# SSD step order, rounding ahead of the activation, a fourth un-normalised feed-forward unit, and a pair part first in odd attention

## The chip, the cores and the metric

The kernel runs on one core of a Trainium2 chip. The metric is the device time of one execution in microseconds, and lower is better.

## The reference, cut to what matters

Two blocks follow one another on 16 + 512 tokens of 1024 channels, all in float32. The parts that the change touches:

```python
def rms_norm(x, g):             # every layer begins with it
    return x * rsqrt(mean(x * x, -1) + eps) * g
# SSD layer: h = rms_norm(x, g); z, x, B, C, dt = h @ w_in; a causal convolution of 4 taps
# over x, B and C, then silu; chunks of 128 tokens with decays exp(-cumsum(dt * exp(a_log)));
# y = (state part + inside part + d_skip * x) * silu(z); per group of 512 channels
# y * rsqrt(mean(y * y) + eps) * gate_norm; x + y @ w_out
# feed-forward: h = rms_norm(x, g); u = h @ w_up; a causal convolution of 3 taps over u;
# x + (silu(gate half) * value half) @ w_down
# odd layer of the second block (16 heads, 4 key groups): compressed blocks, selected
# blocks and a window, each a masked softmax, mixed with three gates
```

## The kernel before, in words

**Storage and number format.** Activations stand transposed, channels on partitions, 528 tokens wide (hT, uT and others in one big tile called arena). Each large product is made as three matmuls in a rounded float32 format (`three`, L683 to L685): high weight times high activation, high weight times the rest of the activation, rest of the weight times high activation. A tile of output is 128 channels by 528 tokens, in two halves, so with 1024 input channels it is 8 x 2 x 3 = 48 matmuls.

**Weights.** A weight unit (128 x 2048, two tiles of 128 columns as a rule) is loaded by SyncE into one of HS = 2 raw slots. ScalarE rounds it (`high_part`, L1306, into arena), and GpSimd subtracts to get the rest (`piece` L2345, `rest` L2336, four operations of 512 columns). Where the last tile of unit h is done, ScalarE rounds unit h + 2.

**SSD order.** `ssd_order` (L62) writes out a list of steps by hand, and every engine walks through the same list and does its own share of each step: `pe_step`, `act_step`, `dve_step`, `pool_step`. There are four groups of eight heads. A group has projections B, C and x (four tiles, each with the convolution on VectorE, L1806 to L1815, and a Silu on ScalarE, L1361), z (four tiles, L1831 and Silu L1365), transposes (`bt` L791, `xt` L824), products (`gram` L801, `l0` L807), states (`st`, L832), and per head a `spread` (L817), `decay` (L1908, L1389), `carry` (L1396, L2380) and `weigh` (L1914). Two heads make a `pair` (L839, L843, L848; L1920, L1924), `low` (L1929) splits its result, `ga` and `gs` add up and sum the gate's squares (L1939, L861), `rc` takes the reciprocal (L1944), and `s` is the output projection (L1837, L1839), which runs inside the next group. Tiles go in turn to two pairs of PSUM banks, PS[0] and PS[1], numbered by SSD_M; a step in OFF_TILE uses none. TensorE may start a tile when VectorE or ScalarE has emptied the one two before it.

**Start.** While uT is made, TensorE multiplies dt, then `stat` sums the squares over channels (L755).

**Feed-forward.** A block has halves of 11 units and 22 tiles. The first FIRST = 3 units use the input without its norm, so that they need not wait for the root of the mean square; VectorE multiplies their output by rstd when it empties the bank (L2025). From then on the input is the normalised one (ul2, uh2), which VectorE and ScalarE make in between (`normalised`, L2001, L2005, L1439), and ScalarE empties the banks (L1429). Each unit has two convolutions of 3 taps (L2029, L2032), a Silu (L1435) and a gated product that is split in two (L2036 to L2041).

**Odd attention.** ODD (L189) is a list of parts: for every two heads five `pair` parts, and one `blocks` part (compressed keys, four heads) ahead of two such pairs. Scores run three parts ahead of transposes. For a blocks part VectorE adds a bias and takes maxima (L2250 to L2259), ScalarE takes the exponential, and GpSimd normalises in three operations (L2448, L2450, L2453) before TensorE transposes (L1202). For a pair part the transposes are L1210.

```python
def act_step(what, g, j):
    ...
    elif what in ("B", "C", "x"):
        ...
        act.wait_ge(sem("sconv_full"), n + 1)
        A(dst, ssd["cv"][:, n % 2, :], ACT.Silu)
    ...
    if what in ("B", "C", "x", "z", "s") and last_of_unit((what, g, j)):
        act.wait_ge(ps_full, M + 1)
        high_part("ssd", 0, SSD_UNIT[what, g, j] + HS)
```

## Time and profile before

| | |
|---|---|
| median of 3 runs | 2463.39 us (2460.68 to 2467.31) |
| the profiled execution | 2468.59 us |
| its span, first to last instruction | 2466.5 us |
| TensorE busy | 2274.3 us, 92% |
| VectorE, ScalarE, GpSimd busy | 52%, 37%, 41% |
| mean granted TensorE clock | 0.96 |

The page of the profile gives busy time, waits and the costliest groups of instructions by line. "PE" is TensorE's matmuls, "PEld" its weight loads, DVE is VectorE, ACT is ScalarE, POOL is GpSimd. A busy TensorE is not one at its peak, since matmuls overlap. "<-" names what ended a wait, and a name with a small q (DVEq) is an engine's sequencer, here mostly a drain in front of a signal. The SSD stage lasts from 0 to about 545 us of the span, the first feed-forward block to about 950, the second from about 1274 to 1680, and odd attention from about 2220 to 2400.

### The profile page before, as it was taken

How to read it: one execution, taken by the hardware profiler on the slowest of the kernel's cores; microseconds unless marked ns; L12 is line 12 of the kernel's file. 1: busy time of each engine (PE TensorE's matmuls, PEld its weight loads, DVE VectorE, ACT ScalarE, POOL GpSimd, SP SyncE). 2: the span in 40 equal slices, each digit the busy share in tenths (PEclk: the TensorE clock that was granted, in tenths of full speed). 3: DMA queues.
4: the chain of work that ended last, by engine and by line, in shares of the span. 5: the costliest groups of instructions: out<-in, count | busy, mean ns of one | idle time of the engine just before them, and what ended most of it. 6: DMA issues, size and time to landing. Idle time of an engine off the chain costs nothing.

```text
span 2466.5 us, 38755 instructions
## 1 busy us (share of the span) xinstructions
PE 2274.3 (92%) x15968; PEld 1982.6 (80%) x15968; DVE 1280.1 (52%) x1919; ACT 921.3 (37%) x1480; POOL 1010.0 (41%) x905
## 2 busy tenths in 40 slices
PE   6889899888999999999998999998998899997887
PEld 6778888778999999985598989976785478885665
DVE  6575757588725735234368716732113551016773
ACT  4362626343313333336532323332224431225661
POOL 3252534334545540022244455544345543435751
PEclk9889998989999999999999999999998999998999
DMA  3111112111222222220012222222221011520100
GB/s 154 52 68 53 69 52 69 52 52 69 76 99 93 83 91 95 85 86 1 1 69 70 86 99 97 78 100 74 84 102 70 18 69 69 156 103 35 35 1 34
DMA packets 29373, 175.59 MB, mean 71 GB/s; under 512 B 3984, under 2 KB 4496, under 8 KB 12304
## 3 DMA queue, kind: packets, MB, share of 16 engines
q1 hardware_dynamic: 29200, 173.14, 19.9%
q8 instruction: 126, 2.06, 0.3%
q14 instruction: 47, 0.39, 0.1%
HBM read 166.71 MB, written 2.10 MB: 68 GB/s over the span
## 4 chain that ended last, share of the span: by engine, by line
PE 68%; DVE 9%; POOL 7%; issue 7%; ACT 2%; POOLq 2%; DVEq 2%; SPq 1%; DMA 0%; ACTq 0%
PE PS L683 20%; PE PS L684 19%; PE PS L685 19%; POOL ring_r L2336 2%; PE PS L960 2%; DVE arena L1815 1%; POOL ring_r L2345 1%; POOL arena L2427 1%; POOL arena L2465 1%; ACT arena_r L1306 1%; DVEq L396 1%; POOLq L2462 1%; PE PD L990 1%; POOL uT L2439 1%; PE PC L960 1%
## 5 line engine op out<-in xcount | busy, mean ns | idle before, releaser
L685 PE MATMUL PS<-arena_r,ring_r 128*128 128x264 f32 (+3 forms) x3728 | 1144.9, 307 | 0.0
L2336 POOL TENSOR_TENSOR ring_r<-ring,arena_r 128x512 fp32r<-128x512 f32 (+1 forms) x456 | 596.1, 1337 | 881.3 <-ACT arena_r L1306 881.3
L685 PEld LDWEIGHTS PS<-arena_r,ring_r 128*128 128x128 f32 x3728 | 714.9, 192 | 31.1
L683 PE MATMUL PS<-arena_r,arena_r 128*128 128x264 f32 (+3 forms) x2288 | 691.6, 302 | 25.7 <-issue 8.8
L684 PE MATMUL PS<-arena_r,arena_r 128*128 128x264 f32 (+2 forms) x2256 | 676.1, 300 | 0.0
L683 PE MATMUL PS<-arena_r 128*128 128x264 f32 (+3 forms) x1792 | 566.0, 316 | 22.2 <-DVEq L396 9.3
L683 PEld LDWEIGHTS PS<-arena_r,arena_r 128*128 128x128 f32 x2288 | 435.3, 190 | 53.7 <-issue 25.5
L684 PE MATMUL PS<-uT_r,arena_r 128*128 128x264 f32 (+2 forms) x1472 | 470.0, 319 | 0.0
L684 PEld LDWEIGHTS PS<-arena_r,arena_r 128*128 128x128 f32 x2256 | 429.7, 190 | 13.0 <-issue 0.2
L1306 ACT ACTIVATE arena_r<-ring 128x2048 fp32r<-128x2048 f32 (+1 forms) x146 | 262.0, 1795 | 419.8 <-PE PS L685 404.8
L683 PEld LDWEIGHTS PS<-arena_r 128*128 128x128 f32 x1792 | 348.4, 194 | 50.8 <-issue 21.4
L684 PEld LDWEIGHTS PS<-uT_r,arena_r 128*128 128x128 f32 x1472 | 287.0, 195 | 17.3
L2345 POOL TENSOR_TENSOR ring_r<-ring,arena_r 128x512 fp32r<-128x512 f32 x128 | 176.7, 1408 | 266.1 <-ACT arena_r L1306 266.1
L1972 DVE TENSOR_TENSOR hT<-hT,PS 128x512 f32<-128x512 f32 (+2 forms) x56 | 38.8, 693 | 239.3 <-PE PS L685 239.1
L2032 DVE SCALAR_TENSOR_TENSOR arena<-arena,par 128x528 f32<-128x528 f32 (+1 forms) x176 | 146.2, 831 | 13.1
L1429 ACT ACTIVATE arena<-PS 128x528 f32<-128x528 f32 (+1 forms) x76 | 46.1, 606 | 280.3 <-PE PS L685 280.3
L1718 DVE TENSOR_TENSOR arena<-PS,sd 128x512 f32<-128x512 f32 (+1 forms) x40 | 27.7, 694 | 223.0 <-PE PS L685 222.8
L2029 DVE TENSOR_SCALAR arena<-arena,par 128x528 f32<-128x528 f32 (+1 forms) x88 | 74.7, 848 | 76.6 <-ACTq L396 71.6
L684 PE MATMUL PS<-ring_r,arena_r 128*128 128x256 f32 x352 | 99.8, 284 | 0.0
L685 PE MATMUL PS<-arena_r,uT_r 128*128 128x256 f32 x320 | 91.0, 284 | 0.0
L1631 ACT ACTIVATE arena<-arena 128x128 f32<-128x128 f32 (+3 forms) x128 | 71.1, 556 | 40.2 <-DVEq L396 35.6
L1815 DVE SCALAR_TENSOR_TENSOR arena<-arena,par 128x528 f32<-128x528 f32 x72 | 72.8, 1010 | 5.4
(329 smaller groups left out, 2827.2 us busy)
## 6 DMA issues: line engine op xcount, KB each, us to landing
ring<-stream SPq DMA_DIRECT2D x130, 1024.0 KB, 4.8
ring<-down SPq DMA_DIRECT2D x32, 704.0 KB, 4.0
hT<-x_in SPq DMA_DIRECT2D x4, 528.0 KB, 7.2
arena<-tables SPq DMA_DIRECT2D x4, 512.0 KB, 3.8
arena<-arena SPq DMA_DIRECT2D x16, 128.0 KB, 2.4
out<-uT SPq DMA_DIRECT2D x4, 512.0 KB, 2.8
par<-params SPq DMA_DIRECT2D x1, 1634.5 KB, 13.9
arena<-arena SPq DMA_DIRECT2D x8, 136.0 KB, 3.3
```

What stands on the lines that cost most here:

```text
L683: mm(out_, r32(ah), r32(bh), start=start, stop=False)
L684: mm(out_, r32(ah), r32(b), start=False, stop=False)
L685: return mm(out_, r32(a), r32(bh), start=False, stop=stop)
L960: return mm(sb_z(u, e)[:, a:a + rhs.shape[1]], w, rhs, start=False, stop=True, skip_group_check=True)
L1306: A(r32(high_slot(h)[:, 0:width]), raw_slot(h)[:, 0:width], ACT.Copy).then_inc(sem("high_full"), 1)
L1429: A(ffn[raw][:, FCONV - 1:FCONV - 1 + n], tile_of(stage, 2 * r + m)[:, first_column(n):first_column(n) + n], ACT.Copy)
L1631: A(x, x, ACT.Exp, bias=od["nm"][:, n % 4, i:i + 1], scale=-1.0, accum_out=od["rs"][:, n % 4, i:i + 1])
L1815: last = V.scalar_tensor_tensor(cv, raw[:, k:k + L], w(k), cv, ALU.mult, ALU.add)
L2029: V.tensor_scalar(out_, ffn[raw][:, 0:width], w(0), b, ALU.mult, ALU.add)
L2032: last = V.scalar_tensor_tensor(out_, ffn[raw][:, k:k + width], w(k), out_, ALU.mult, ALU.add)
L2336: last = G.tensor_tensor(r32(low[:, cut]), raw[:, cut], split(high[:, cut]), ALU.subtract)
L2345: last = G.tensor_tensor(r32(low[:, cut]), raw[:, cut], split(high[:, cut]), ALU.subtract)
```

## The change

1. In the first group B runs ahead of `stat`, and dt's product stands in PD, which makes it a step without a tile. z(0,1) runs ahead of l0.
2. At the end of groups 0 to 2, z(g+1,0) and bt(g+1) run ahead of the last pair. Behind it come gram, ga, low, l0, z(g+1,1) and only then gs; rc stands behind xt(1). In the last group z(3,3) runs ahead of the states, and the s tiles are dealt out anew.
3. ScalarE rounds the next weights in front of a step's activation, not behind it (SSD stage only).
4. FIRST is 4. VectorE empties tile 2(r+1) ahead of unit r's gated product and tile 2(r+1)+1 behind it, and makes the normalised input in portions of 4, 2 and 2 channel blocks, where it was 4 and 4.
5. The first two entries of ODD change places, so pair part (0,0) is ahead of the first blocks part; and the sums ahead of the loop are arranged to fit.

```diff
-FIRST = 3
+FIRST = 4
...
+        then = [("z", g + 1, 0), ("bt", g + 1, 0)] if g + 1 < GROUPS else []
...
-        return out + [("pair", g, HPG // 2 - 1)]
+        return out + then + [("pair", g, HPG // 2 - 1)]
...
-    order = [("dt", 0, 0), ("stat", 0, 0)] + projections(0) + [("dtt", 0, 0), ("z", 0, 0), ("end", 0, 0)]
-    order += [("bt", 0, 0), ("gram", 0, 0), ("l0", 0, 0), ("z", 0, 1), ("xt", 0, 0), ("xt", 0, 1), ("xt", 0, 2)]
+    order = [("dt", 0, 0), ("B", 0, 0), ("stat", 0, 0)] + projections(0)[1:] + [("dtt", 0, 0), ("z", 0, 0), ("end", 0, 0)]
+    order += [("bt", 0, 0), ("gram", 0, 0), ("z", 0, 1), ("l0", 0, 0), ("xt", 0, 0), ("xt", 0, 1), ("xt", 0, 2)]
...
-        order += z[0] + [("ga", g - 1, 0), ("low", g - 1, 3), ("bt", g, 0), ("gs", g - 1, 0), ("gram", g, 0), ("l0", g, 0)]
-        order += [("rc", g - 1, 0)] + z[1] + [("xt", g, 0), ("xt", g, 1)] + z[2] + [("xt", g, 2), ("spread", g, 0), ("spread", g, 1)]
+        order += [("gram", g, 0), ("ga", g - 1, 0), ("low", g - 1, 3), ("l0", g, 0)] + z[1] + [("gs", g - 1, 0)]
+        order += [("xt", g, 0), ("xt", g, 1), ("rc", g - 1, 0)] + z[2] + [("xt", g, 2), ("spread", g, 0), ("spread", g, 1)]
+        order += z[3]
         if last:
-            order += [("decay", g, 0)] + states(g, dict(enumerate(s[0:3])))
-            order += through(g, {0: z[3], 1: s[3], 2: s[4], 3: s[5], 5: s[6], 7: s[7]})
+            order += [("decay", g, 0)] + states(g, {0: s[0], 2: s[1]})
+            order += through(g, {0: s[2], 1: s[3], 2: s[4], 3: s[5], 5: s[6], 7: s[7]})
         else:
...
-            order += z[3] + [("decay", g, 0)] + states(g, {0: s[0], 1: s[1] + B, 2: s[2], 3: s[3] + C})
+            order += [("decay", g, 0)] + states(g, {0: s[0], 1: s[1] + B, 2: s[2], 3: s[3] + C})
...
-OFF_TILE = ("spread", "decay", "weigh", "carry", "low", "ga", "gs", "rc", "stat")
+OFF_TILE = ("spread", "decay", "weigh", "carry", "low", "ga", "gs", "rc", "stat", "dt")
...
+ODD[0], ODD[1] = ODD[1], ODD[0]
...
+        dt_sums = PD[:, :, :].rearrange("p a b -> p (a b)")[:, V0:V0 + L]
...
-                            last = mm(t[0:32, V0 + a:V0 + b], w_dt[:, k, :], hT[:, k, a:b], start=k == 0, stop=k == KD - 1)
-                    last.then_inc(ps_full, 1)
+                            last = mm(dt_sums[0:32, a:b], w_dt[:, k, :], hT[:, k, a:b], start=k == 0, stop=k == KD - 1)
+                    last.then_inc(sem("dt_full"), 1)
...
+                if what in ("B", "C", "x", "z", "s") and last_of_unit((what, g, j)):
+                    act.wait_ge(ps_full, M + 1)
+                    high_part("ssd", 0, SSD_UNIT[what, g, j] + HS)
...
-                if what in ("B", "C", "x", "z", "s") and last_of_unit((what, g, j)):
-                    act.wait_ge(ps_full, M + 1)
-                    high_part("ssd", 0, SSD_UNIT[what, g, j] + HS)
...
-                        if half == 0 and r < 2:
-                            for k in range(4 * r, 4 * r + 4):
+                        if half == 0 and r < 3:
+                            for k in range(2 * r + 2 if r else 0, 2 * r + 4):
                                 act.wait_ge(sem("n_raw"), 8 * i + k + 1)
                                 A(r32(uh2[:, k, 0:n], NORMED), sq[:, k % 2, 0:n], ACT.Copy).then_inc(sem("nh_full"), 1)
...
-                    dve.wait_ge(ps_full, dt_M + 1)
-                    V.tensor_tensor(dtv, PS[dt_M % 2][0:32, V0:V0 + L], rstd[0:32, :], ALU.mult)
+                    dve.wait_ge(sem("dt_full"), 1)
+                    V.tensor_tensor(dtv, dt_sums[0:32, :], rstd[0:32, :], ALU.mult)
...
-                    signal(dve, sem("dtv_full"), ps_free[dt_M % 2])
+                    signal(dve, sem("dtv_full"))
...
                         V.tensor_tensor(GA, squares(g, 0), squares(g, 1), ALU.add)
+                        dve.drain()
...
+                def scale(r, m):
+
+                    dve.drain()
+                    tile_wait(dve, f"ffn{i}a", 0, 2 * R, 2 * r + m)
+                    v0 = first_column(width)
+                    V.tensor_tensor(ffn[("rawg", "rawv")[m]][:, FCONV - 1:FCONV - 1 + width],
+                                    tile_of(f"ffn{i}a", 2 * r + m)[:, v0:v0 + width], rstd[:, 0:width], ALU.mult)
+                    signal(dve, free_of(f"ffn{i}a", 2 * r + m))
+
+                scale(0, 0)
...
+                        early = half == 0 and r + 1 < FIRST
...
@@ -2018,19 +2034,16 @@
                             n = raw_tile(i, half, r, m)
                             if n >= 0:
                                 dve.wait_ge(raw_full, n + 1)
-                            else:
-                                dve.drain()
-                                tile_wait(dve, stage, 0, 2 * R, 2 * r + m)
-                                v0 = first_column(width)
-                                V.tensor_tensor(ffn[raw][:, FCONV - 1:FCONV - 1 + width],
-                                                tile_of(stage, 2 * r + m)[:, v0:v0 + width], rstd[:, 0:width], ALU.mult)
-                                signal(dve, free_of(stage, 2 * r + m))
+                            elif (r, m) == (0, 1):
+                                scale(r, m)
                             out_ = ffn[cv][:, 0:width]
                             V.tensor_scalar(out_, ffn[raw][:, 0:width], w(0), b, ALU.mult, ALU.add)
                             for k in range(1, FCONV):
                                 dve.drain()
                                 last = V.scalar_tensor_tensor(out_, ffn[raw][:, k:k + width], w(k), out_, ALU.mult, ALU.add)
                             last.then_inc(conv_full, 1)
+                        if early:
+                            scale(r + 1, 0)
...
-                        if half == 0 and r < 2:
-                            normalised(4 * r)
-                            normalised(4 * r + 2)
+                        if early:
+                            if r == 0:
+                                normalised(0)
+                            scale(r + 1, 1)
+                            normalised(2 * r + 2)
...
-            odd_sum(0)
-            for n in range(2):
-                odd_scale(n)
+            odd_scale(0)
+            odd_sum(1)
```

The order in the boundary from group 0 to group 1 on VectorE. L1920 and L1924 are the last pair, L1831 empties a z tile, L1939 is ga, L1865 and L1867 are gram, L1872 l0, L1944 the reciprocal. Before:

```order
L1933 TENSOR_TENSOR arena<-arena 128x528
L1920 SCALAR_TENSOR_TENSOR arena<-arena,par,PS 128x528
L1924 TENSOR_TENSOR arena<-arena 128x528
L1831 TENSOR_TENSOR arena<-PS,sd 128x528
L1939 TENSOR_TENSOR arena<-arena 128x528 x2
L1929 SCALAR_TENSOR_TENSOR arena_r_51<-arena,par,arena_r_51 128x528
L1865 TENSOR_TENSOR arena<-PS,par 16x16
L1867 TENSOR_TENSOR arena<-PS,par 128x512
L1872 TENSOR_TENSOR arena<-PS,arena 16x128
L1876 TENSOR_SCALAR arena<-arena 16x128
L1944 RECIPROCAL arena<-arena 128x528
```

And now (the same lines are 4 or 5 higher: L1835 z, L1924 and L1928 the pair, L1869 and L1871 gram, L1944 ga, L1876 l0):

```order
L1937 TENSOR_TENSOR arena<-arena 128x528
L1835 TENSOR_TENSOR arena<-PS,sd 128x528
L1924 SCALAR_TENSOR_TENSOR arena<-arena,par,PS 128x528
L1928 TENSOR_TENSOR arena<-arena 128x528
L1869 TENSOR_TENSOR arena<-PS,par 16x16
L1871 TENSOR_TENSOR arena<-PS,par 128x512
L1944 TENSOR_TENSOR arena<-arena 128x528 x2
L1933 SCALAR_TENSOR_TENSOR arena_r_51<-arena,par,arena_r_51 128x528
L1876 TENSOR_TENSOR arena<-PS,arena 16x128
L1880 TENSOR_SCALAR arena<-arena 16x128
L1835 TENSOR_TENSOR arena<-PS,sd 128x528
```

The emptying of z went ahead of the last pair, gram went ahead of ga, and the reciprocal left this place.

The rounding (L1306 before, L1311 now) on ScalarE in the middle of group 0, beside the Silu of tile x(1,1) (L1361, now L1370), with the exponentials of a decay (L1389, now L1398) behind. Before:

```order
L1389 ACTIVATE arena<-arena 128x128 x4
L1396 ACTIVATE arena<-PC 128x512
L1361 ACT_TABLE_LOAD
L1361 ACTIVATE arena<-arena 128x528
L1306 ACTIVATE arena_r_52<-ring 128x2048
L1389 ACT_TABLE_LOAD
L1389 ACTIVATE arena<-arena 128x128 x4
L1396 ACTIVATE arena<-PC 128x512
```

And now:

```order
L1398 ACTIVATE arena<-arena 128x128 x4
L1405 ACTIVATE arena<-PC 128x512
L1311 ACTIVATE arena_r_52<-ring 128x2048
L1370 ACT_TABLE_LOAD
L1370 ACTIVATE arena<-arena 128x528
L1398 ACT_TABLE_LOAD
L1398 ACTIVATE arena<-arena 128x128 x4
L1405 ACTIVATE arena<-PC 128x512
```

The rounding went ahead of the load of the Silu's table and of the Silu.

The first unit of a feed-forward block on VectorE. L2025 (now L2020) empties a tile times rstd, L2029 and L2032 (now L2040 and L2043) are the convolution, L2036 to L2041 (now L2049 to L2054) the gated product, L2001 and L2005 (now L2006 and L2010) the normalised input. Before:

```order
L2025 TENSOR_TENSOR arena<-PS,sd 128x528
L2029 TENSOR_SCALAR arena<-arena,par 128x528
L2032 SCALAR_TENSOR_TENSOR arena<-arena,par 128x528 x2
L2036 TENSOR_TENSOR arena<-arena 128x528
L2039 CAST arena_r_51<-arena 128x528
L2041 TENSOR_TENSOR arena_r_51<-arena,arena_r_51 128x528
L2001 SCALAR_TENSOR_TENSOR sq<-hT,par,sd 128x528 x2
L2005 TENSOR_TENSOR arena_r_53<-sq,arena_r_53 128x528 x2
L2001 SCALAR_TENSOR_TENSOR sq<-hT,par,sd 128x528 x2
L2005 TENSOR_TENSOR arena_r_53<-sq,arena_r_53 128x528 x2
L2025 TENSOR_TENSOR arena<-PS,sd 128x528
```

And now:

```order
L2020 TENSOR_TENSOR arena<-PS,sd 128x528
L2040 TENSOR_SCALAR arena<-arena,par 128x528
L2043 SCALAR_TENSOR_TENSOR arena<-arena,par 128x528 x2
L2020 TENSOR_TENSOR arena<-PS,sd 128x528
L2049 TENSOR_TENSOR arena<-arena 128x528
L2052 CAST arena_r_51<-arena 128x528
L2054 TENSOR_TENSOR arena_r_51<-arena,arena_r_51 128x528
L2006 SCALAR_TENSOR_TENSOR sq<-hT,par,sd 128x528 x2
L2010 TENSOR_TENSOR arena_r_53<-sq,arena_r_53 128x528 x2
L2020 TENSOR_TENSOR arena<-PS,sd 128x528
L2006 SCALAR_TENSOR_TENSOR sq<-hT,par,sd 128x528 x2
L2010 TENSOR_TENSOR arena_r_53<-sq,arena_r_53 128x528 x2
```

Tile 2 is emptied ahead of the gated product, where it was emptied behind all four blocks of normalised input, and tile 3 between the two portions.

## Rows read from the trace of the kernel before

**Rows 1.** The page, its first part: busy time, share of the span, instructions

```profile
PE 2274.3 (92%) x15968; PEld 1982.6 (80%) x15968; DVE 1280.1 (52%) x1919; ACT 921.3 (37%) x1480; POOL 1010.0 (41%) x905
```

**Rows 2.** Busy time by stage: stretch, length, each engine, granted clock, DMA

```profile
0.00:545.00 545.00, 463.55 (x3608) 424.50 (x3608) 366.02 (x474) 253.72 (x371) 211.18 (x156) 0.93 0.19 68
545.00:625.00 80.00, 71.67 (x539) 70.89 (x540) 65.72 (x73) 22.69 (x25) 31.41 (x20) 0.92 0.20 72
625.00:1270.00 645.00, 638.66 (x4954) 580.65 (x4953) 305.70 (x424) 237.38 (x388) 218.75 (x240) 1.00 0.21 72
```

**Rows 3.** TensorE's waits: line, releaser, us in total, times, longest

```profile
PE PC L1202 <- POOL arena L2453: 16.9, 4, 7.4
PE PS L683 <- DVEq L396: 15.9, 12, 4.1
...
PE PC L861 <- DVE arena L1939: 13.4, 4, 4.0
PE PS L683 <- POOL ring_r L2345: 10.8, 4, 5.7
...
PE PS L839 <- DVE arena L1920: 4.7, 3, 2.1
```

**Rows 4.** Busy time in a stretch of the feed-forward at full clock

```profile
612.00:625.00 13.00, 13.00 (x110) 13.00 (x109) 9.84 (x10) 3.80 (x4) 6.17 (x4) 1.00 0.31 108
```

**Rows 5.** Timeline of the start: start, us, engine and line, [idle before <-releaser]

```profile
25.04 2.13 PE L755 MATMUL PC<-sd,par 128*128 128x264 f32 x4 [8.37 <-DVEq L398]
...
37.63 1.28 ACT L1361 ACT_TABLE_LOAD   x1
38.92 0.65 ACT L1361 ACTIVATE arena<-arena 128x528 f32<-128x528 f32 x1
...
45.40 1.90 ACT L1306 ACTIVATE arena_r<-ring 128x2048 fp32r<-128x2048 f32 x1
...
53.67 0.39 PE L683 MATMUL PS<-arena_r 128*128 128x264 f32 x1 [2.60 <-POOL ring_r L2345]
```

**Rows 6.** Timeline, l0's matmuls

```profile
82.09 1.84 PE L807 MATMUL PS<-acs_parts,pick 96*128 96x16 f32 x8 [3.74 <-DVEq L396]
```

**Rows 7.** Timeline, a pair in the middle of group 0

```profile
155.32 1.97 PE L843 MATMUL PS<-arena 128*64 128x128 f32 x16 [2.84 <-DVE arena L1914]
...
159.10 1.98 PE L848 MATMUL PS<-arena 128*64 128x128 f32 x16 [1.81 <-POOL arena L2380]
```

**Rows 8.** Timeline, the boundary from group 1 to 2

```profile
287.75 1.98 PE L843 MATMUL PS<-sq,arena 128*64 128x128 f32 x16 [1.11 <-DVE sq L1914]
...
298.36 2.31 DVE L1939 TENSOR_TENSOR arena<-arena 128x528 f32<-128x528 f32 x2 [0.28 <-issue]
...
300.82 1.64 PE L861 MATMUL PC<-arena,par 128*128 128x264 f32 x4 [2.93 <-DVE arena L1939]
```

**Rows 9.** Timeline, an s tile in the last group

```profile
474.92 0.59 PE L683 MATMUL PS<-arena_r,arena_r 128*128 128x264 f32 x1 [5.66 <-POOL ring_r L2345]
```

**Rows 10.** Timeline, the first feed-forward block's start

```profile
571.06 0.56 PE L683 MATMUL PS<-arena_r 128*128 128x264 f32 x1 [4.14 <-DVEq L396]
...
588.63 0.56 PE L683 MATMUL PS<-arena_r,arena_r 128*128 128x264 f32 x1 [4.16 <-issue]
```

**Rows 11.** Busy time there: up to the first normalised tile; one unit

```profile
551.50:588.60 37.10, 28.83 (x223) 28.43 (x223) 32.59 (x39) 13.15 (x14) 12.64 (x8) 0.95 0.16 58
570.10:581.80 11.70, 10.74 (x76) 10.77 (x77) 10.05 (x11) 1.63 (x2) 6.43 (x4) 0.85 0.23 90
```

**Rows 12.** Timeline, odd attention's first transposes

```profile
2237.61 1.09 PE L1202 MATMUL PC<-par,arena 128*128 128x128 f32 x4 [7.39 <-POOL arena L2453]
```

**Rows 13.** Busy time in a stretch at the lower granted clock

```profile
420.70:431.10 10.40, 10.40 (x49) 9.73 (x48) 4.62 (x5) 3.58 (x4) 0.00 (x0) 0.51 0.21 86
```

**Rows 14.** The convolution's instruction: its group on the page, and durations

```profile
L1815 DVE SCALAR_TENSOR_TENSOR arena<-arena,par 128x528 f32<-128x528 f32 x72 | 72.8, 1010 | 5.4
...
L1815 DVE SCALAR_TENSOR_TENSOR arena<-arena,par x72: 768/770/1667, 35.1 to 410.2; 128x528 f32<-128x528 f32 x72
```

1 line of the change is left out of this document (removed).

## The prediction

> **What bounds it now.** I read the page's totals first, then a table by stage, then TensorE's waits, then the places of the longest. TensorE is busy 92% of a span of 2466.5 us [rows 1], and the stages differ: from 625 to 1270 us it is idle 6 of 645 us at a granted clock of 1.00. In the SSD stage (0 to 545) it is busy 463.6 of 545 at 0.93, and in the first 80 us of the feed-forward block 71.7 at 0.92 [rows 2]. So TensorE sets the end wherever work is there for it, and what the change can win is its idle time, plus what the lower clock behind idle time costs. VectorE is a near second only in the feed-forward start: 65.7 of 80 us. The waits with a cause that repeats are a sum over channels that VectorE hands over late (L861, four times, 13.4 us), weights that GpSimd has not split yet (L683 behind L2345, 10.8), PSUM tiles that VectorE has not emptied (L683 behind a drain, 15.9), and attention's first transposes (L1202) [rows 3]. The change aims at all four.
>
> The profiled execution took 2468.59 us, 5.2 over the median of 2463.39. The sum is made against the profiled one, and the same difference is then taken from the median. A measurement of this kernel can tell about 0.3%, 7 us, from no change.
>
> **Part 1, the start.** TensorE waits 8.37 us in front of the statistics' matmul, while VectorE makes uT piece by piece. Tile B needs just these pieces and fits into that wait; its last piece is there less than a microsecond before the sum is. The statistics then come about half a microsecond later, and C, x0 and x1 move up by a tile, which is 48 matmuls at 13/110 = 0.12 us, with its start 5.9 us [rows 4]. The gain does not arrive whole: banks are emptied behind the dt chain. What decides is x2, which starts at 53.67 behind GpSimd's split, and that behind ScalarE's rounding at 45.40, which waited for C's Silu. B's Silu ends at 39.6 [rows 5]; with the rounding in front of C's Silu and half a microsecond for the later statistics it starts at 40.1, and x2 5.3 us earlier. dt's sum in a bank of its own costs nothing: that bank is not used before the decays. **5.3 us.**
>
> **Part 2, z(0,1) in front of l0.** TensorE idles 3.74 us until VectorE has split the running sums into three parts [rows 6]. A z tile of 5.9 us now stands there, its weights the same unit as z(0,0)'s. **3.7 us.**
>
> **Part 3, rounding in front of the Silu.** In the middle of group 0 a pair waits 2.84 us for a weigh step, whose exponentials stood behind a rounding, and then 1.81 for a carry product that stood on GpSimd behind a split [rows 7]. The rounding needs the tile and not its convolution, so it comes up to a convolution earlier, about 3 us (three L1815 of 0.77 [rows 14] and one scaling). The second wait goes, and the first shrinks by the 1.9 us of the rounding: **3.5**. Groups 1 and 2 wait 2.1 us each for the pair's bank (L839, 4.7 us in three) [rows 3], behind convolutions that run beside a split; a split that is over earlier may free them or hit others, so I take half: **2.0**, bounds 0 and 4.2.
>
> **Part 4, the boundaries.** Three times TensorE waits for the gate's sum, 13.4 less the last group's 3.5, and, in two groups, 1.11 us inside the last pair [rows 3, 8]. Now z(g+1,0) and bt stand in front of that pair, which hides the 1.11. Between the pair and the sum stood z and bt, 6.7 us; now gram, l0 and z(g+1,1) stand there, about 9, and ga (L1939, 298.36) no longer stands behind the emptying of z on VectorE. Both together cover the 2.93 us, and nearly the longest, 4.0. So 9.9 + 2.2 = **12.1**. The reciprocal, 3.45 us on VectorE, moves behind xt(1), where z2's matmuls cover it; without that cover z3's bank would come late by its length. ScalarE gets one table load more, 1.28 us (37.63), and its next activation starts 0.01 us behind it (38.92) [rows 5]: beside TensorE's work, nothing. The last group's sum keeps its wait, since its tail is not reordered.
> The Trainium skill (ScalarE: Activation LUTs, What ACT_TABLE_LOAD costs) adds a drain of about 1.38 us to every switch. By that the added load would take 2.7 us of ScalarE; the row behind the load shows no such time.
>
> **Part 5, last group.** z(3,3) moves ahead of the states, so its unit's rounding is no longer late, and the wait of 5.66 us for a split goes [rows 9]. Late next is the first pair's decay and carry, with three s tiles (3 us each, half a z) above it where z, s and the wait stood; I see no new wait over 1 us. **5.7 us.**
>
> **Part 6, feed-forward, twice.** TensorE waits 4.14 us for an emptied bank and then 4.16 for bank and normalised input [rows 10]. Tile 2 ends at 561.0 (571.06 - 4.14 - 5.9) and is now emptied at once, not at 570.9, so the first wait goes. The second needs VectorE's work counted. Up to the end of normalising it does eight scales, six convolutions, three gatings and four normalised pairs, before it five, four, two and four: 32.6 us busy of 37.1. One unit with two scales, two convolutions and gating is 10.05 [rows 11], a further scale 0.7, so 43.4 us; at the same share busy 49 us, up to 601. TensorE could be at the last piece of the ninth tile at 566.9 + 4.9 x 5.9 = 596. Following both queues, I get 1.3 us of wait at tile 6, 2.3 and 0.6 at tile 8 and about 1 at tile 10, whose rounding stands behind the last copies on ScalarE: 5.2 us in place of 8.3, and about 1 less if a split meets fewer of the operations. **4 each, 8.0**; bounds 0 and 8.3 each. From the fifth unit on nothing changes.
>
> **Part 7, attention.** The first transposes wait 7.39 us for GpSimd's three operations of a "blocks" part [rows 12]. With pair (0,0) in front, its transposes and the next scores, some 3.5 us, run first; but the blocks chain starts behind pair 0 on VectorE, about 1 us later. **2.5 us**, bounds 0 and 6.
>
> **The clock.** Behind such waits the granted clock falls to its lower level, 1.2 of 2.4 GHz: 0.51 from 420.7 to 431.1, behind the third gate sum, where 49 matmuls take 10.4 us, 0.21 each [rows 13]. Eleven stretches of this kind lie behind waits named above, 54 us together. At half speed, with TensorE at some 87% in them, they cost 23. Where waits of 1 to 2 us stay it may still fall; I take half: **12 us**.
>
> **The sum.** 5.3 + 3.7 + 5.5 + 12.1 + 5.7 + 8.0 + 2.5 = 42.8 of idle time and 12 of clock: 54.8. Every cover that is used up bares what is late next. Now ten short waits of about 0.8 us stand in front of L683 for banks alone (15.9 less 4.1 and 4.0) [rows 3]; I take as many new ones off, 8 us. That is 47: a span near 2420, and a median of 2463.4 - 47 = **2416 us**.
>
> **Rivals.**
> - **Collision: slower.** L1815 takes 770 ns alone and up to 1667 beside GpSimd [rows 14]. Its mean of 1010 (72.8 us in 72) says that (1010 - 770)/0.90 = 19 of 72 were hit. The rounding in front puts the split onto the same tile's convolution. If all 72 and the 32 weigh steps are hit, VectorE gets 85 x 0.90 = 76 us more. It goes slower once 61 of the 85 lie on TensorE's path, the price of the 54.8; with all of them the time is 2463 + 76 - 55 = 2484. Against it: the splits are as many as before, moved by 3 us in a rhythm of two tiles, 12 us, and convolutions now cost TensorE 2 us a group. 4%.
> The Trainium skill (SBUF — State Buffer, SBUF: two separate sides) speaks against the change here: the port pair is an exclusive lock, so a VectorE operation with two SBUF inputs waits for the whole GpSimd instruction that holds it. The trace agrees in kind (1667 against 770), and doesn't say how many would meet.
> - **Given back: no change.** 50 of the 85 on the path (45 us) and part 6 lost: 2463 - 55 + 45 + 8 = 2461. 4%.
> - **VectorE bounds the feed-forward start, and the clock stays low.** Parts 6 and 7 and the clock give nothing: 42.8 - 10.5 - 8 = 24, time 2439. For it: VectorE at 82% there [rows 2]. 17%.
> - **All waits go and the clock holds.** 42.8 + 12 (the bounds of parts 3, 6) + 23, with no new waits: 78, time 2385. 11%.
> - Forecast: 64%, its own range 2400 to 2432.
>
> The range that leaves out no more than 2 in 10 is 2391 to 2445. Faster by over 0.3%: 92%; within it: 4%; slower: 4%.
>
> **What would show it.** B's matmuls in the place of the 8.37 us wait and x2 near 48; no wait over 1 us at the l0 matmuls; the gate sum without a wait three times, and the fourth with 3.5 still; no wait over 2 us for a split; the first wait gone in each feed-forward block, with waits of 1 to 3 us at tiles 6, 8 and 10; the transposes' wait near 4; L1815's mean under 1150 ns; the mean clock up from 0.96 to about 0.97. It is wrong if L1815's mean passes 1300 with waits behind L1806 and L1831, or if a feed-forward start still loses 8 us.

## The result, and the profile after

The changed kernel takes **2442.28 us** (median of four runs, 2435.57 to 2444.41) against 2462.98 for the kernel before (median of four, 2460.68 to 2467.31): ratio 0.9912, 95% interval 0.9892 to 0.9932. That is 20.7 us faster. The time lies inside the forecast range (2391 to 2445), but the gain is less than half of the 47 us that were forecast.

The profiled execution of the changed kernel took 2435.57 us, 6.7 under its median; that of before took 2468.59, 5.2 over its own. The two profiles therefore differ by 33 us and the medians by 21. Twelve of the 33 are the two executions and not the change. One execution of the kernel e12_front_two_groups below took 3128 us at a granted clock of 0.65 and is left out of its median.

Line numbers have moved: L683 is now L688, L839 is L844, L843 is L848, L861 is L866, L1815 is L1819, L1929 and L1933 (the low half and the gate's first sum) are L1933 and L1937, and L2345 is L2359. The page's first part, for [rows 1]:

```profile
PE 2260.2 (93%) x15968; PEld 1969.5 (81%) x15968; DVE 1298.7 (53%) x1923; ACT 920.6 (38%) x1477; POOL 1019.2 (42%) x905
```

The table by stage, for [rows 2] (stretch, length, each engine's busy time, granted clock, DMA):

```profile
0.00:522.12 522.12, 451.44 (x3608) 413.94 (x3608) 380.38 (x474) 256.14 (x372) 220.32 (x156) 0.97 0.20 71
522.12:602.00 79.88, 73.41 (x546) 72.23 (x547) 68.27 (x75) 21.86 (x24) 30.78 (x20) 0.92 0.22 80
602.00:1245.00 643.00, 636.68 (x4951) 579.82 (x4950) 306.14 (x425) 237.17 (x387) 219.02 (x240) 1.00 0.20 71
```

The SSD stage went from 545 to 522.1 us with the same 3608 matmuls. TensorE's idle time there (length less busy time, as everywhere below) fell from 81.5 to 70.7 us, so 10.8, and its busy time from 463.6 to 451.4, so 12.1: that is the granted clock, 0.93 before and 0.97 now. VectorE is busy 14.4 us *more* in the stage, for 474 instructions as before.

TensorE's waits up to 522 us, for [rows 3] (line, releaser, us in total, times, longest):

```profile
PE PS L688 <- DVEq L399: 14.4, 12, 2.3
PE PS L844 <- DVEq L401: 9.9, 3, 4.2
...
PE PC L866 <- DVE arena L1944: 3.5, 1, 3.5
PE PS L844 <- DVE arena L1924: 3.3, 3, 2.4
PE PS L688 <- POOL ring_r L2359: 3.3, 3, 1.3
```

Most of what was to go has gone. Of four waits for the gate's sum the last is left (3.5 us). The waits for a split fell from 10.8 to 3.3 us, and the 3.74 us at l0 and the 8.37 us at the statistics are no longer there. (In the middle of group 0, 2.4 and 1.1 us are left of the 2.84 and 1.81 in [rows 7].) But there is a new group, second in size: L844, the first matmuls of the last pair of a group, 9.9 us in three. Before, the last pair waited for its bank 2.1 us each in groups 1 and 2 and 0.5 in the last (L839 in [rows 3]), behind the pair product; now it is 2.8, 4.2 and 2.8 in groups 0, 1 and 2, behind another step. The longest, at the boundary from group 1 to 2, in the timelines of TensorE, VectorE and GpSimd (start, us, engine, line, [idle before it]):

```profile
284.81 0.29 PE L844 MATMUL PS<-arena 16*64 16x16 f32 x4 [4.24 <-DVEq L401]
...
275.33 0.71 DVE L1810 TENSOR_TENSOR arena<-PS,sd 128x528 f32<-128x528 f32 x1
276.16 0.55 DVE L1816 TENSOR_SCALAR arena<-arena,par 128x528 f32<-128x528 f32 x1
276.79 3.33 DVE L1819 SCALAR_TENSOR_TENSOR arena<-arena,par 128x528 f32<-128x528 f32 x3
280.05 1.77 DVE L1933 SCALAR_TENSOR_TENSOR arena_r<-arena,par,arena_r 128x528 fp32r<-128x528 f32 x1
281.74 1.76 DVE L1937 TENSOR_TENSOR arena<-arena 128x528 f32<-128x528 f32 x1
283.57 0.71 DVE L1835 TENSOR_TENSOR arena<-PS,sd 128x528 f32<-128x528 f32 x1
...
278.04 6.58 POOL L2359 TENSOR_TENSOR ring_r<-ring,arena_r 128x512 fp32r<-128x512 f32 x4 [1.65 <-ACT arena_r L1311]
```

Read it backwards. The pair waits for its PSUM bank. The banks go in turn, and in the new order its bank is that of z(2,0), two steps earlier. z(2,0) is emptied at 283.57 (L1835), because VectorE first has x3's convolution, the low half of pair 2 and the gate's first sum to do. These three ran beside a GpSimd split, and three instructions took 1.65 to 1.77 us instead of 0.70 to 0.77. The split starts 1.3 us behind the convolution's first instruction at 276.79, since the rounding in front of x3's Silu released it; with the rounding behind the Silu it starts 5.0 us behind it (below, 280.59 against 275.58).

A second new wait, 2.24 us in group 1 and 2.25 in group 2, comes the same way. The C tile's convolution meets a split, 4.20 us for three instructions instead of 2.46, and the emptying of an s tile stands behind it on VectorE:

```profile
233.51 0.36 PE L688 MATMUL PS<-arena_r,arena_r 128*128 128x264 f32 x1 [2.24 <-DVEq L399]
...
225.23 4.20 DVE L1819 SCALAR_TENSOR_TENSOR arena<-arena,par 128x528 f32<-128x528 f32 x3
...
225.68 6.78 POOL L2359 TENSOR_TENSOR ring_r<-ring,arena_r 128x512 fp32r<-128x512 f32 x4 [0.81 <-ACT arena_r L1311]
```

### The profile page after: what moved, and what is told of

Its sections match the earlier page's. It is cut to its first block, busy times and chain, and to the rows that moved or that the text cites. A ratio compares the mean times of both kernels' runs of the same rounds, so it can differ in the third digit from the quotient of the medians.

```text
span 2433.6 us, 38757 instructions
## 1 busy us (share of the span) xinstructions
PE 2260.2 (93%) x15968; PEld 1969.5 (81%) x15968; DVE 1298.7 (53%) x1923; ACT 920.6 (38%) x1477; POOL 1019.2 (42%) x905
## 4 chain that ended last, share of the span: by engine, by line
PE 63%; DVE 13%; issue 7%; POOL 6%; DVEq 3%; ACT 3%; POOLq 2%; SPq 1%; DMA 0%; ACTq 0%
PE PS L688 19%; PE PS L689 18%; PE PS L690 18%; DVE arena L1819 3%; POOL ring_r L2350 2%; PE PS L965 2%; DVE arena L2043 1%; POOL arena L2441 1%; POOL arena L2479 1%; POOLq L2476 1%; DVEq L399 1%; PE PD L995 1%; ACT arena_r L1311 1%; POOL uT L2453 1%; PE PC L965 1%
## 5 line engine op out<-in xcount | busy, mean ns | idle before, releaser
L688 PE MATMUL PS<-arena_r,arena_r 128*128 128x264 f32 (+3 forms) x2224 | 674.2, 303 | 25.5 <-DVEq L399 10.3
L689 PE MATMUL PS<-arena_r,arena_r 128*128 128x264 f32 (+3 forms) x2192 | 658.6, 300 | 0.0
L688 PE MATMUL PS<-arena_r 128*128 128x264 f32 (+3 forms) x1856 | 580.7, 313 | 22.9 <-DVEq L399 8.0
L689 PE MATMUL PS<-uT_r,arena_r 128*128 128x264 f32 (+3 forms) x1536 | 485.9, 316 | 0.0
L688 PEld LDWEIGHTS PS<-arena_r,arena_r 128*128 128x128 f32 x2224 | 423.5, 190 | 54.3 <-issue 30.5
L1311 ACT ACTIVATE arena_r<-ring 128x2048 fp32r<-128x2048 f32 (+1 forms) x146 | 262.2, 1796 | 465.7 <-PE PS L690 451.4
L689 PEld LDWEIGHTS PS<-arena_r,arena_r 128*128 128x128 f32 x2192 | 418.1, 191 | 12.9 <-issue 0.2
L688 PEld LDWEIGHTS PS<-arena_r 128*128 128x128 f32 x1856 | 356.8, 192 | 52.7 <-issue 22.2
L689 PEld LDWEIGHTS PS<-uT_r,arena_r 128*128 128x128 f32 x1536 | 296.5, 193 | 17.3
L2359 POOL TENSOR_TENSOR ring_r<-ring,arena_r 128x512 fp32r<-128x512 f32 x128 | 187.3, 1492 | 219.3 <-ACT arena_r L1311 219.3
L2043 DVE SCALAR_TENSOR_TENSOR arena<-arena,par 128x528 f32<-128x528 f32 (+1 forms) x176 | 158.4, 900 | 13.5 <-issue 0.4
L2040 DVE TENSOR_SCALAR arena<-arena,par 128x528 f32<-128x528 f32 (+1 forms) x88 | 78.4, 891 | 66.6 <-ACTq L399 62.2
L1819 DVE SCALAR_TENSOR_TENSOR arena<-arena,par 128x528 f32<-128x528 f32 x72 | 80.1, 1112 | 5.4
## 6 DMA issues: line engine op xcount, KB each, us to landing
par<-params SPq DMA_DIRECT2D x1, 1634.5 KB, 14.1
```

What stands on the lines that cost most here:

```text
L688: mm(out_, r32(ah), r32(bh), start=start, stop=False)
L689: mm(out_, r32(ah), r32(b), start=False, stop=False)
L1311: A(r32(high_slot(h)[:, 0:width]), raw_slot(h)[:, 0:width], ACT.Copy).then_inc(sem("high_full"), 1)
L1819: last = V.scalar_tensor_tensor(cv, raw[:, k:k + L], w(k), cv, ALU.mult, ALU.add)
L2040: V.tensor_scalar(out_, ffn[raw][:, 0:width], w(0), b, ALU.mult, ALU.add)
L2043: last = V.scalar_tensor_tensor(out_, ffn[raw][:, k:k + width], w(k), out_, ALU.mult, ALU.add)
```

## The experiments

Two theories stood at the start. **T**: the saved time came back as waits for banks behind VectorE's queue in front of the last pair. **R**: the rounding in front moved GpSimd's splits onto VectorE's work just where a bank is wanted. **C** was the rival that it was all clock and luck of the run. All kernels were timed beside the kernel before, in three batches (its medians in them 2461.92, 2464.05 and 2460.95 us). "Idle" is TensorE's idle time up to the first feed-forward statistics, from the table of busy time; before has 81.5. (The expectations count it differently: that of e1_again without the first 7.9 us of the program, the later ones without the last wait, 4.2 us.) e1 to e4, e5 to e8 and e9 to e12 shared a batch each. Where kernels of two batches are compared, the difference is given by the medians and by the ratios. The intervals of e2, e6, e7 and e8 overlap that of e1_again, so for these the idle time has to bear the reading out.

| kernel | us | ratio to before, 95% | idle |
|---|---|---|---|
| e1_again | 2439.99 | 0.9903, 0.9886 to 0.9920 | 71.2 |
| e2_round_behind | 2432.26 | 0.9881, 0.9862 to 0.9899 | 66.0 |
| e3_boundary_old | 2451.63 | 0.9956, 0.9940 to 0.9972 | 75.5 |
| e4_low_behind | 2430.53 | 0.9866, 0.9847 to 0.9885 | 64.4 |
| e5_front_start_only | 2426.19 | 0.9842, 0.9819 to 0.9866 | 62.8 |
| e6_ffn_old | 2444.26 | 0.9910, 0.9889 to 0.9932 | 71.3 |
| e7_start_old | 2445.17 | 0.9920, 0.9901 to 0.9940 | 76.2 |
| e8_odd_old | 2438.47 | 0.9896, 0.9876 to 0.9917 | 69.1 |
| e9_low1_behind_pair | 2426.05 | 0.9851, 0.9827 to 0.9874 | 62.9 |
| e10_rounding_alone | 2465.82 | 1.0013, 1.0000 to 1.0027 | 81.1 |
| e11_boundary_alone | 2443.59 | 0.9925, 0.9906 to 0.9943 | 68.1 |
| e12_front_two_groups | 2428.00 | 0.9861, 0.9835 to 0.9886 | 62.7 |

### The changed kernel again (no edit)

> The changed kernel once more, unedited, for its idle time and its clock in a second profile. Theory T (the idle time that the new order saved at the boundaries came back as waits of TensorE for PSUM banks behind VectorE): the idle time in front of TensorE's matmuls up to the feed-forward statistics is the same as in the first profile, 62 to 64 us, with the last pair of groups 0, 1 and 2 waiting about 10 us together; time 2439 to 2445. Rival C (it is the clock: its gain came in the first profile by luck of that run): the idle time is the same too, but the granted clock of the whole span is 0.965 or less and the stretch that the change does not touch, 350 us behind the first feed-forward start, is as long as in the kernel before.

Measured: 2439.99 us, 22 below before. The idle time is 71.2 (70.7 in the first profile) and the three pairs wait 9.9 us again. The middle stage, which the change does not touch, took 643.63 us here, exactly as long as in the profile of before, and 641.95 in the first profile of the changed kernel (three rows of the table by stage: this run, the first profile, before):

```profile
605.95:1249.58 643.63, 637.32 (x4943) 579.45 (x4942) 305.11 (x423) 236.36 (x387) 218.88 (x240) 1.00 0.21 71
...
602.90:1244.85 641.95, 635.63 (x4943) 578.77 (x4942) 305.32 (x423) 236.21 (x387) 219.02 (x240) 1.00 0.20 71
...
626.83:1270.46 643.63, 637.29 (x4942) 579.28 (x4942) 304.78 (x423) 236.42 (x387) 218.75 (x240) 1.00 0.20 71
```

So C holds for a part of the first profile, and only of it: the whole span's clock is 0.967, where C asked for 0.965 or less. In this profile TensorE's busy time in the SSD stage is 454.6, 9.0 below before: most of the clock's share is real.

### The rounding back behind the activation

The same three lines, taken from the head of ScalarE's step and put at its end:

```diff
-                if what in ("B", "C", "x", "z", "s") and last_of_unit((what, g, j)):
-                    act.wait_ge(ps_full, M + 1)
-                    high_part("ssd", 0, SSD_UNIT[what, g, j] + HS)
...
+                if what in ("B", "C", "x", "z", "s") and last_of_unit((what, g, j)):
+                    act.wait_ge(ps_full, M + 1)
+                    high_part("ssd", 0, SSD_UNIT[what, g, j] + HS)
```

> The changed kernel with the rounding of the next weights back behind the activation (part 3 undone, all else kept). Theory T: the convolution's mean (now 1.11 us) hardly moves, the last pair of three groups still waits 8 us or more, and the waits of 2.8 and 1.8 in the middle of group 0 come back: 2 to 6 us slower than the changed kernel. Rival R (the rounding in front puts GpSimd's split on the same tile's convolution, and this is what filled the saved time): the convolution's mean falls to about 1.01, the last pairs' waits fall from 9.9 to under 4, and the time is 3 to 8 us below the changed kernel's.

Measured: 2432.26 us, 7.7 **faster** than the changed kernel measured beside it (5.4 by the ratios), with 5.2 us less idle time. R's numbers came: the convolution's mean fell from 1112 to 989 ns and the last pairs' waits from 9.9 to 2.0 us. One part of the change costs more than it brings. The same place in this kernel, the boundary from group 1 to 2:

```profile
272.77 0.36 PE L688 MATMUL PS<-arena_r 128*128 128x264 f32 x1 [2.21 <-DVE arena L1924]
...
280.64 0.29 PE L844 MATMUL PS<-arena 16*64 16x16 f32 x4 [1.25 <-DVEq L401]
...
263.97 5.06 DVE L1819 SCALAR_TENSOR_TENSOR arena<-arena,par 128x528 f32<-128x528 f32 x3
...
275.58 2.46 DVE L1819 SCALAR_TENSOR_TENSOR arena<-arena,par 128x528 f32<-128x528 f32 x3
277.95 0.76 DVE L1933 SCALAR_TENSOR_TENSOR arena_r<-arena,par,arena_r 128x528 fp32r<-128x528 f32 x1
278.63 0.70 DVE L1937 TENSOR_TENSOR arena<-arena 128x528 f32<-128x528 f32 x1
...
262.30 6.17 POOL L2359 TENSOR_TENSOR ring_r<-ring,arena_r 128x512 fp32r<-128x512 f32 x4 [3.98 <-ACT arena_r L1311]
...
280.59 2.50 POOL L2359 TENSOR_TENSOR ring_r<-ring,arena_r 128x512 fp32r<-128x512 f32 x2 [5.40 <-ACT arena_r L1311]
```

The split ahead of this one, released behind x1's Silu, now meets x2's convolution, 5.06 us for three instructions instead of 2.46 (in the changed kernel x1's took 4.21 and x2's 3.34). The tile that waits 2.21 us for it at 272.77 is z(2,0): x3's matmuls ended at 270.56, and z(2,0) takes the bank that pair 2's product (L1924) empties, the bank for which the last pair waited 2.1 us before the change. x3's own convolution, the low half and the sum run at full speed, and the pair waits 1.25 us instead of 4.24. The collision isn't avoided; it stands a tile earlier, where less hangs on it. At the start it is the other way round: without the rounding in front, x2's split is late, and much more so than in the old order:

```profile
52.75 0.59 PE L688 MATMUL PS<-arena_r 128*128 128x264 f32 x1 [6.17 <-POOL ring_r L2359]
```

### The old order at the boundaries and in the last group

```diff
-        then = [("z", g + 1, 0), ("bt", g + 1, 0)] if g + 1 < GROUPS else []
...
-        return out + then + [("pair", g, HPG // 2 - 1)]
+        return out + [("pair", g, HPG // 2 - 1)]
...
-        order += [("gram", g, 0), ("ga", g - 1, 0), ("low", g - 1, 3), ("l0", g, 0)] + z[1] + [("gs", g - 1, 0)]
+        order += z[0] + [("ga", g - 1, 0), ("low", g - 1, 3), ("bt", g, 0), ("gs", g - 1, 0), ("gram", g, 0), ("l0", g, 0)]
```

> The changed kernel with the old order at the boundaries and in the last group (parts 4 and 5 undone, start, rounding and feed-forward kept). As forecast these parts are worth 12.1 + 5.7 = 18 us: 2460. Theory T: the 9.9 us in front of the last pairs go and the gate sums' 9 to 10 us and the last group's split wait (up to 5.7) come back, so that only 2 to 8 us are lost: 2444 to 2450. Rival R: if the rounding in front already moved the last group's split, that wait is under 2 us here, and the time is within 3 us of the changed kernel.

Measured: 2451.63 us, 11.6 slower than e1_again: more than T, less than the forecast's 18. The gate sums wait 11.3 us in four again, and the split in the last group 3.6 instead of 5.7, since the rounding in front had already taken 2.0 off it. The idle time rose by only 4.3 us, TensorE's busy time by 12.3 (454.55 to 466.80 for the same matmuls): three quarters of the 16.5 us that this stage lost are clock. 4.7 of the 16.5 came back behind the stage, where the two profiles run the same instructions, so the clock's share of the loss is not settled by them.

```profile
0.00:542.25 542.25, 466.80 (x3608) 426.76 (x3608) 378.92 (x474) 254.67 (x371) 218.39 (x156) 0.94 0.19 69
```

### VectorE's queue cleared in front of z's emptying

```diff
-            elif e > 1:
+            elif e > 1 and e + 1 < HPG:
                 out += [("low", g, e // 2 - 1)]
-        return out + then + [("pair", g, HPG // 2 - 1)]
+        return out + then + [("low", g, 2), ("pair", g, HPG // 2 - 1)]
...
-                    if j == 2:
+                    if j == (2 if g == GROUPS - 1 else 1):
                         dve.wait_ge(sem("gsq_full"), 4 * g + 2)
                         V.tensor_tensor(GA, squares(g, 0), squares(g, 1), ALU.add)
```

The first sum must go up as well, as it reads the squares that lie in z's place.

> The changed kernel with VectorE's queue cleared ahead of the emptying of z(g+1,0): the low half of pair 2 goes behind it, and the gate's first sum goes up two heads, behind low 1. Same work on each engine. Theory T: the three waits of 2.8, 4.2 and 2.8 us in front of the last pair shrink to 0 to 2 each, 5 to 8 us together, and the time is 4 to 9 us below the changed kernel. Rival R (the convolution itself is late, because it meets the split): the waits shrink by less than 3 us together and the time stays within 3 us.

Measured: 2430.53 us, 9.5 faster than e1_again, with every engine's work unchanged. Each of the three waits (9.9 us) is 0.38 us now, and 0.92 us stands at z(2,0), ahead of one of them; the idle time fell by 6.8. The convolution still meets the split:

```profile
276.97 0.36 PE L688 MATMUL PS<-arena_r 128*128 128x264 f32 x1 [0.92 <-DVE arena L1924]
...
283.97 0.29 PE L844 MATMUL PS<-arena 16*64 16x16 f32 x4 [0.38 <-DVEq L401]
...
279.77 3.32 DVE L1819 SCALAR_TENSOR_TENSOR arena<-arena,par 128x528 f32<-128x528 f32 x3
283.08 0.71 DVE L1835 TENSOR_TENSOR arena<-PS,sd 128x528 f32<-128x528 f32 x1
```

T is shown: TensorE paid for the queue in front of the emptying. But e2, which left the queue and moved the split, took 7.9 of the 9.9 us away as well, though z(g+1,0) waits 5.0 us in two groups there. The last pair's wait takes both, queue and split, and either one undone is enough to end most of it.

### The rounding in front at the start only

Beside the edit of e4_low_behind:

```diff
+                front = what in ("B", "C", "x") and g == 0
+                if rounds and front:
+                    round_next()
...
+                if rounds and not front:
+                    round_next()
```

> The rounding in front of the activation for the tiles B, C and x of group 0 alone, behind it for all others, and the low half of pair 2 and the gate's first sum moved as in e4_low_behind. Theory R (the rounding in front is worth its 5.4 us at the start, where it takes away the wait of 6.17 for x2, and costs elsewhere, because GpSimd's split then meets VectorE's work before the last pair): idle time of the stage up to the feed-forward statistics 54 to 57 us against 61.8 of e2_round_behind and 60.2 of e4_low_behind, time 2423 to 2428, below all others. Rival B (the two mends overlap: with the last pair's wait gone by either, and the start's wait moved on to the next late bank): idle time 59 or more, time 2430 or more.

Measured: 2426.19 us, the fastest together with e9; the idle time, 58.6 in the expectation's measure, lies between its two cases. Against e1_again it is 13.8 us faster by the medians and 15.0 by the ratios. The 6.17 us are gone, the last pairs wait under 1 us. But z(g+1,0) now waits 3.0 and 3.5 us in groups 1 and 2, because the gate's first sum, moved up, now stands in front of the pair 2 product that empties its bank (x3's matmuls ended at 269.53):

```profile
272.55 0.56 PE L688 MATMUL PS<-arena_r 128*128 128x264 f32 x1 [3.02 <-DVE arena L1931]
```

### The old feed-forward start, the old start, the old odd attention

The three edits put back the lines of the diff above that belong to parts 6, 1 and 2, and 7 (`FIRST = 3` with its loops; dt, B and l0; `ODD` unswapped).

> The changed kernel with the old feed-forward start (part 6 undone). As forecast part 6 is worth 8 us, 4 per block: 2448. From the two profiles it is worth 1.8 us of idle time in the first block and 1.9 in the second: 2442 to 2446, with idle times of 12.5 and 12.1 us around the two starts against 10.7 and 10.2. Rival (VectorE's extra work up to the normalised input eats it all): within 2 us of the changed kernel, or faster.

Measured: 2444.26 us, over e1_again by 4.3 by the medians and 1.7 by the ratios. The waits of 4.14 and 4.20 are back in the first block; with the change there are four, 2.01, 1.34, 0.59 and 2.53, at tiles 6, 8, 8 and 10. So part 6 saved 1.8 us of idle time in the first block. In the profiles of before and after the second block's waits went from 8.1 to 6.2.

> The changed kernel with the old start (parts 1 and 2 undone: dt's sum in the shared bank, B behind the statistics, l0 before z(0,1)), the rounding still in front. As forecast these parts are worth 5.3 + 3.7 = 9 us: 2449, with the waits of 8.4 in front of the statistics and 3.7 at l0 back. Rival (x2's split decides, and the rounding in front brings it forward in the old order as well, so that B's place is worth little): 2443 to 2445.

Measured: 2445.17 us, over e1_again by 5.2 by the medians and 4.2 by the ratios; idle time 5.0 more. The waits of [rows 5, 6] (8.37 and 3.74) are back, with the l0 wait shorter:

```profile
25.09 2.13 PE L758 MATMUL PC<-sd,par 128*128 128x264 f32 x4 [8.21 <-DVEq L401]
...
78.48 1.84 PE L810 MATMUL PS<-acs_parts,pick 96*128 96x16 f32 x8 [2.65 <-DVEq L399]
```

> The changed kernel with the old order of odd attention's first parts (part 7 undone). Forecast: worth 2.5 us. The two profiles say 0.6 us: within 2 us of the changed kernel, the 7.4 us wait at the first transposes back, and the waits of 2.1, 2.1 and 1.4 behind them gone. Rival (the new order costs, since the blocks part stands a microsecond later on VectorE): 1 to 3 us faster than the changed kernel.

Measured: 2438.47 us, under e1_again by 1.5 by the medians and 1.7 by the ratios, with overlapping intervals: no difference shown, and none of the 2.5 us. In place of one wait of 7.55 us the new order has three, 5.6 together, for the first pair's reads, for the blocks part, and later (timeline of the changed kernel):

```profile
2201.18 1.12 PE L1215 MATMUL PC<-par,arena 128*128 128x128 f32 x4 [2.08 <-DVE arena L2309]
...
2206.42 1.09 PE L1207 MATMUL PC<-par,arena 128*128 128x128 f32 x4 [2.11 <-POOL arena L2467]
...
2218.77 1.07 PE L1215 MATMUL PC<-par,arena 128*128 128x128 f32 x8 [1.44 <-issue]
```

### Low 1 behind the pair, and two groups in front

Against e5_front_start_only:

```diff
-                out += [("pair", g, e // 2 - 1)]
-            elif e > 1 and e + 1 < HPG:
-                out += [("low", g, e // 2 - 1)]
+                out += [("pair", g, e // 2 - 1)] + ([("low", g, 1)] if e == 6 else [])
+            elif e == 3:
+                out += [("low", g, 0)]
```

> e5_front_start_only with one more step moved on VectorE: the low half of pair 1 and the gate's first sum go behind the pair 2 product, which empties the bank that the tile x3 waits for. Theory Q (the waits of 3.0 and 3.5 us in front of x3 in groups 1 and 2 are VectorE's queue, 1.8 + 0.7 us of which needn't stand there): they fall to about 1 each, idle time of the stage 54 to 55 us against 58.6, time 2419 to 2424. Rival: the wait only moves on, to the last pair or to z(g+1,0), since VectorE has the same work to do: idle time 57.5 or more, time within 3 us of 2426.

Measured: 2426.05 us and the same idle time as e5. The rival was right: at the end of group 1 z(2,0) (the expectation calls it x3) waits 1.6 us instead of 3.0, and the last pair 2.0 and z(2,1) behind it 1.0, where they waited for 0.4 and 0.7. VectorE has the same work between these banks in both orders, and the wait only moved on.

> e9_low1_behind_pair with the rounding in front for the tiles B, C and x of groups 0 and 1, so also in the loop of group 0. For it: the waits of 2.8 and 2.7 us in the middle of group 0 become 2.5 and 1.1. Against it: the split then stands on x3's convolution in front of z(1,0). Within 2 us of e9_low1_behind_pair as idle time; the sign tells whether the rounding in front is to be kept at the start only.

Measured: 2428.00 us, idle time within 0.3 of e9. The middle of group 0 gains 1.0 us (2.52 and 1.11 in place of 2.83 and 1.80), and the last pair of group 0 waits 2.85 again. It decides nothing.

### The rounding alone and the boundary alone

Each is the kernel before with only that part of the diff.

> The kernel before with the rounding in front of the activation alone (part 3 and nothing else). Forecast: 5.5 us faster than before, 2457 or so. Theory R (the rounding in front helps only where a split is late, in group 0, and its splits meet VectorE's work in front of late banks): idle time of the stage within 3 us of the 77.3 of before, time within 4 us of before. Rival: worth more than forecast, over 8 us, because clock stretches go too.

Measured: 2465.82 us, ratio 1.0013 (1.0000 to 1.0027): no gain, where 5.5 were forecast. The idle time is 0.3 less. The 2.6 us in front of x2 are gone, and so are the 2.1 us of the last pairs of groups 1 and 2; the last group's split costs 3.6 us and not 5.7. But the 4.65 us in the middle of group 0 fell by 1.1 only, new waits of 2.25 us stand at s tiles in groups 1 and 2, and three of 0.7 to 0.8 in front of bt:

```profile
152.24 0.29 PE L839 MATMUL PS<-arena 16*64 16x16 f32 x4 [2.40 <-DVE arena L1920]
153.65 1.32 PE L843 MATMUL PS<-arena 128*64 128x128 f32 x16 [1.11 <-DVE arena L1914]
...
245.58 0.36 PE L683 MATMUL PS<-arena_r,arena_r 128*128 128x264 f32 x1 [2.25 <-DVEq L396]
```

> The kernel before with the new order at the boundaries and in the last group alone (parts 4 and 5), the rounding behind the activation as before. Theory R (these parts are sound, and it is together with the rounding in front that they lose): 15 to 20 us faster than before, waits in front of the last pairs under 2 us each. Theory T alone (VectorE's queue in front of z(g+1,0)'s emptying costs this whatever the rounding does): last pairs wait 8 us or more together, 8 to 12 us faster than before.

Measured: 2443.59 us, 17.4 below before, so parts 4 and 5 by themselves bring most of what the whole change brings. The last pairs of groups 0 to 2 wait 0.38 us each; their old 2.1 us stand at z(g+1,0) now, which takes the bank behind pair 2's product, 2.2 in two groups. The waits for a bank behind VectorE in its list are 7.7 and 4.4 us, against 14.4 and 9.9 in the changed kernel:

```profile
PE PS L685 <- DVEq L398: 7.7, 8, 2.3
...
PE PS L685 <- POOL ring_r L2348: 4.8, 3, 2.3
PE PS L685 <- DVE arena L1922: 4.4, 2, 2.2
```

The busy time of its SSD stage: idle 68.1 us, 13.4 less than before, and 457.94 busy, 5.6 less.

```profile
0.00:526.04 526.04, 457.94 (x3608) 421.34 (x3609) 366.11 (x474) 254.92 (x372) 211.61 (x156) 0.94 0.19 71
```

## Why the prediction was right in its signs and wrong in its size

Nearly every sign that the prediction named came. B's matmuls stand in the place of the 8.37 us and x2 starts near 48; the gate sum waits once and not four times; no split is waited for over 2 us; the convolution's mean is 1112 ns, under 1150; the mean clock rose from 0.96 to 0.97. In the SSD stage only one of them looked at a wait that the new order makes, the last: waits behind L1806 and L1831. It was tied to a convolution's mean over 1300, and the waits behind L1831 (now L1835) came at 1112. Over the whole span the idle time fell from 192.2 to 173.4 us, by 18.8 where 42.8 - 8 = 34.8 were forecast, and TensorE's busy time by 14.1 where 12 were (17.1 and 10.2 in e1_again). So what fell short is the idle time.

- **Parts 1 and 2, 5.3 + 3.7 us forecast.** Worth 4.2 to 5.2 together (e7). The waits went, and two of 1.5 and 1.8 us for banks, which stood nowhere before, came in behind them.
- **Part 3, the rounding in front, 5.5 us forecast.** This is the step that failed. It is worth nothing alone (e10) and costs 7.7 us inside the change (e2; 5.4 by the ratios). Of the 3.5 us in the middle of group 0, 1.1 came. The prediction let the split "be over earlier" and took half of the 4.2 us of group 1 and 2 as a gain. It did not walk the moved split through VectorE's queue. The old 2.1 us behind the pair product did go, but the moved split meets the convolution, the low half and the first sum in front of the last pair, 9.9 us in three, and the C tile's convolution in front of an s tile, 4.5 us in two groups. 28 of the 72 convolution instructions take over 1.2 us, 20 before and 18 with the rounding behind: few more hits, but in other places. At the start the rounding in front is right, and worth 5.4 us of a wait that part 1 would otherwise bare (6.17 in e2, 0.78 in the changed kernel).
- **Parts 4 and 5, 12.1 + 5.7 us forecast.** Alone they brought 17.4 us (e11). That is near the 17.8 partly by luck: the terms are idle time, of which 13.4 came, and the rest is clock, which the forecast counted apart. With the rounding in front they brought 11.6 (e3). The prediction put z(g+1,0) in front of the last pair as a cover and saw its matmuls alone. It missed that the pair takes z's bank, that z's emptying stands last in VectorE's queue, and that z takes the bank that pair 2's product empties, for which the pair waited before. Clearing that queue gave 9.5 us back (e4).
- **Part 6, 8.0 us forecast.** 1.7 to 4.3 (e6). The mechanism was right, and even the places: the first wait went, and VectorE's share of work makes new waits at tiles 6, 8 and 10. Their sum was 6.5 us in the first block and not 5.2, since tile 10 waits 2.5 us and not 1.
- **Part 7, 2.5 us forecast.** Nothing that can be shown (e8).
- **The clock, 12 us forecast.** It came: 9.0 and 12.1 us of busy time in the SSD stage in two profiles. The size is partly luck: the half of the 23 us was a guess. It is not in proportion to idle time, though: e3 has 6 us less idle time than before and 3.2 us more busy time.
- **The 8 us taken off for new short waits.** The size was wrong. The terms of the SSD stage say 32.3 us, and most of the waits they name went; the idle time fell by 10.8. So some 21 us of new waits stand in this stage alone. 17.7 of them are the 9.9, 4.5 and 3.3 us above.

The rival "collision", given 4%, named the mechanism that took the gain, and was dismissed as all or none: it asked for 61 hits on the path. Eight more on the convolution, with those on the low halves and first sums, were enough to take all of part 3's gain and some of part 4's, because of where they stood. The upper rival's 12 us for the bounds of parts 3 and 6 are 10.8 by its own numbers (2.2 and 2 x 4.3). The rival of an idle feed-forward part gave nearly the measured time, 2439, by a mechanism that did not happen: part 6 and the clock both gave something. The Trainium skill (SBUF — State Buffer, SBUF: two separate sides) says that a VectorE operation contends with GpSimd when it has two SBUF inputs or runs in a two-port mode. The traces agree on the inputs: inside the split from 278.04 to 284.62, L1937 with two inputs from SBUF took 1.76 us (0.70 alone), and L1835, one of whose inputs is PSUM, took 0.71.

What stays open: the undone parts add up to less than the whole (5.2 - 7.7 + 11.6 + 4.3 - 1.5 = 11.9 of 22 us). The parts share waits and clock, and no run here splits that remainder. The best versions, e5 and e9, are 37.9 and 34.9 us below before in their own batches; which of the two is faster wasn't settled. Neither was the old odd attention tried together with them.

## What to carry to other kernels

When a step is put in front of another as a cover, follow its bank as well as its matmuls: who empties it, what stands in that engine's queue, and who takes the bank next. Rounding or splitting ahead moves a collision rather than removing it, so walk the moved work through the neighbour engine's queue at each place, and keep the move only where it pays, here at the start. A part that looks like a small term is worth a run of its own: one of 5.5 us turned out at 0 alone and at -7.7 beside the others.

## What the runs showed of the hardware that was not expected

The same 3608 matmuls of the SSD stage took from 445.8 (e12) to 466.8 us (e3) of busy time. These 21 us are the granted clock (0.98 and 0.94 in the stage), larger than the differences in idle time between most of the orders: of the stage, 73 us stand at the lower level before, 65 in e3, 32 in the changed kernel's first profile and 21 in e12. They don't follow the sum of the waits; whether their places decide is not shown. A kernel with less idle time can lose by the clock what it won: e4 has 1.7 us less than e2 and 6.6 more busy time. One profile is too little to price it: two profiles of the same program differ by 3 us in this stage. Beside a split, GpSimd pays too: its pieces took 1.49 us on average in the changed kernel, 1.41 before.
